# A two-layer diffusion block with mixture of experts: context key and query columns made directly transposed, one modulation product moved between the layers, and a leaner hand-over at the end of the experts

## The chip, the cores and the metric

The kernel runs on one core of one Trainium2 chip. The metric is the device time of one execution in microseconds (us); lower is better. Everything is fp32. The profile is one execution of the same program, read from its trace.

## What is computed

256 latent tokens (x) and 256 context tokens (ctx), 1024 wide, go through two layers. In the last layer only the latent tokens are carried on. Cut to what matters here:

```
for l in range(2):
    mod, modc = silu(c) @ w_ada[l] + b_ada[l], silu(c_ctx) @ w_ada[l] + b_ada[l]   # 6 x 1024 each
    h, hc = rmsnorm(x) * (1 + mod[1]) + mod[0], the same for ctx with modc
    qa, ka, va, qb, kb, vb, uc = split(h @ w_in[l]);  the same for hc
    rotary embedding of qa, ka, qb, kb, for the latent tokens only
    o_a = differential attention (4 heads), o_b = windowed attention with sinks (4 heads), o_c = conv module of uc
    x = x + mod[2] * (concat(o_a, o_b, o_c) @ w_out[l]);  layer 0: the same for ctx
    h2 = rmsnorm(x) * g_ffn * (1 + mod[4]) + mod[3]
    y = 16 experts (1024 -> 512 -> 1024), 2 per token
    x = x + mod[5] * y
out = rmsnorm(x, g_final)
```

The keys and queries of the context tokens get no rotary embedding: they go from the product to the attention as they are.

## The kernel before

Work on the five engines is written out by hand and kept in step by semaphores; between stages all engines but SyncE pass a barrier (`barrier`: drain the engine, raise `phase`, wait until four engines have done so; `pass_barrier` on GpSimd is the same without the drain). One layer is this series of stages:

1. **Columns of h** (barrier 1). VectorE scales X by the row norms into YS. TensorE transposes YS, eight groups named `nT`; VectorE and ScalarE evict them with scale and shift into HT, which holds h with features on the partitions.
2. **Input products** (barrier 2), in the order of `in_jobs`: uc, ka, b, va, qa. Weight segments of 2 MB lie in a ring of six slots. A job of ka, b or qa is one tile of 128 tokens: eight matmuls with HT stationary and 512 weight columns moving. Its result has tokens on the partitions, but scores need features there, so it is put into a staging tile ST (by VectorE with the rotary embedding for tiles 0 and 1, by ScalarE's L949 as a plain copy for the context tiles 2 and 3), transposed by TensorE (`transposes`, L1682, one job later) and copied by ScalarE (`copy_T`, L918) into kT or qT. Jobs of uc are made the other way round: weights stationary, HT moving, features on the partitions.
3. **Attention** (barrier 3): units of one query tile and one pair of heads, 24 in layer 0 and 12 in layer 1. `attention_steps` writes the order out: scores S two units ahead, the transposes T of the probabilities (L1770), the outputs O of the unit before. Between S and T `fill` puts up to three steps of "dense" work: in layer 0 first the three modulation products (1, 0), (1, 1), (1, 2) of layer 1 ("A" steps, `ada_part`, four matmuls of 128x32 on 128x512 each, eight steps a product), then the output products ("W") of query tiles whose heads are done. Units 0 to 2 carry product (1, 0), units 3 to 5 carry (1, 1), units 6 to 8 carry (1, 2); W begins at unit 9.
4. **Routing** (barrier 4), and then the **experts** (barrier 5): per expert 6 MB of weights through nine slots, and a loop over blocks of 32 tokens. GpSimd gathers block n (L830) and scatters the result of block m (L838). Each scatter first waits for the result, then copies its list of rows (L836), then starts its DMA.
5. **Combine**: ScalarE loads the scattered rows, two DMAs for each token tile (L1069), VectorE adds the two, multiplies by the gate and adds to X (L1589, L1591, L1593), ScalarE and GpSimd make the norms, VectorE makes YS of the next layer (L1139).

A modulation product (l, q) makes 2048 of the 6144 modulation columns for both conditions. Its weights come in four loads of 2 MB, `front_units`; VectorE adds the bias (`mod_rows`, L1115), GpSimd stores the rows to DRAM (`store_mod`) and other engines load them back. (1, 1) holds the attention gate and the shift of the second norm of layer 1, which are first needed after barrier 2 of layer 1.

SyncE's queue has all weight loads in order. At the end of layer 0 it issues the last expert's loads, two gate loads (L704), then waits for the combine's second tile, and then loads layer 1's segments (L650). A load also waits until its slot was freed by TensorE.

Of the kernel before, what the change touches and what calls it, by code (L numbers as in the profile page):

```python
# [43 lines left out]
EXTRA = 3 * GROUPS - RING  # L44

# [75 lines left out]
def bank_plan():  # L121
# [13 lines left out]
    for l in range(DEPTH):  # L135
        nq = TILES if l == 0 else 2
        for g in range(8):
            if l == 0 and g == 4:
                for key in (("par",), ("cw",), ("ada", 0, 0), ("modc", 0)):
                    put(key)  # L140
            put(("nT", l, g))
        prev = None
        for job in in_jobs(l):
# [3 lines left out]
            prev = job if job[0] in ("ka", "b", "qa") else None  # L147
# [65 lines left out]

def quad_after(l, job):
# [7 lines left out]
def front_units(l):  # L222

    out = [("ada", 0, j) for j in range(4)] if l == 0 else []
# [6 lines left out]
    if l == 0:  # L231
        out += [("ada", 1, j) for j in range(4 * QUADS)]
# [13 lines left out]
def attention_steps(l):  # L246
# [4 lines left out]
    dense = ([("A", q) for q in range(QUADS)] if l == 0 else []) + [("W", i, h) for i in range(nq - 1) for h in range(OUT_N)]  # L251
# [41 lines left out]
def hybrid_moe_kernel(nc, A):  # L293
# [4 lines left out]
    with ctx:  # L298
# [69 lines left out]
        def mst_of(key):  # L368
# [4 lines left out]
            return acc[:, 0 if q == 0 else 1, 0:CHUNK]  # L373
# [189 lines left out]
        def bar(l, k):  # L563
            return 5 * l + k
# [6 lines left out]
        MODS = [(l, q) for l in range(DEPTH) for q in range(QUADS)]  # L571

        def bias_of(n):
            return bias0 if n == 0 else bias12[:, n % 2] if n < QUADS else G[:, 1, 0:CHUNK]
# [70 lines left out]
        def _(sp):  # L645
# [8 lines left out]
            for l in range(DEPTH):  # L654
                for name in front_units(l):
                    if name[0] == "ada":
# [48 lines left out]
                if l < DEPTH - 1:  # L705

                    sp.wait_ge(y_in[1], 32 * (l + 1))
# [3 lines left out]
        def _(pool):  # L711
# [48 lines left out]
            for l in range(DEPTH):  # L760
# [28 lines left out]
                if l == 0:  # L789
                    pool.wait_ge(mod_sb, QUADS + 1)  # L790
                    load_bias(QUADS + 1)
                    pool.wait_ge(mod_sb, QUADS + 2)
                    store_mod(QUADS + 1)
                    load_bias(QUADS + 2)
                else:
                    load_ffn_rows(l)
                for i in range(nq):
                    if l == 0 and i == 1:
                        pool.wait_ge(mod_sb, QUADS + 3)
                        store_mod(QUADS + 2)  # L800
                        pool.wait_ge(ab_done, 2)
                        for q in range(1, QUADS):
                            pool.wait_ge(mod_out[1, q], 64)
# [16 lines left out]
                def gather(n, r, made_=0):  # L820
# [4 lines left out]
                    if isinstance(n, int):  # L825
# [1130 lines left out]
```

## Time and profile before

| | us |
|---|---|
| median of 3 runs | 1211.78 (1206.96 to 1214.02) |
| the profiled execution, its own time | 1216.56 |
| its span in the trace | 1214.8 |
| TensorE busy, share of the span | 971.6, 80% |
| TensorE weight loads | 529.7, 44% |
| VectorE busy | 464.1, 38% |
| ScalarE busy | 257.1, 21% |
| GpSimd busy | 224.5, 18% |
| mean granted TensorE clock | 0.897 of full speed |
| DMA | 317.92 MB, mean 262 GB/s |

A busy share is a mean over stages with different limits. The stages lie as follows: layer 0 until about 360 us up to its routing, its experts until 690, combine and layer 1's start until 725, layer 1's products and attention until about 900, its experts until 1190, and the final combine.

### The profile page before, as it was taken

What the parts mean: (1) busy time and instruction counts of PE and PEld (TensorE: products, weight loads), DVE (VectorE), ACT (ScalarE), POOL (GpSimd) and SP (SyncE); (2) the same over time, 40 slices, a digit from 0 to 9 for tenths busy, and PEclk for the clock granted to TensorE, in tenths of its full rate; (3) what the DMA queues carried; (4) which work ended last, traced back from release to release, by engine and by line L of the source; (5) the groups of instructions that cost most, each with busy time, mean ns of one, the idle gap of its engine ahead of it and who ended that gap; (6) DMA issues with size and microseconds to landing.
All of it is one profiled execution on the core that took longest, in us unless ns stands there. A gap on an engine that the chain in (4) does not pass through costs nothing. (4 is left out here: it accounts for less than half of the span.)

```text
span 1214.8 us, 23396 instructions
## 1 busy us (share of the span) xinstructions
PE 971.6 (80%) x8536; PEld 529.7 (44%) x8537; DVE 464.1 (38%) x1008; ACT 257.1 (21%) x497; POOL 224.5 (18%) x364
## 2 busy tenths in 40 slices
PE   3899999999889399999989429998887397755880
PEld 1344444355446255555545225543554254322440
DVE  1159505555535433333323166606633422211233
ACT  2100112343312022222212020113511122111110
POOL 2100000121001124333433230000000123211331
PEclk9699999999987599999989869999988598877895
DMA  9966612995003668999999196115007299999983
GB/s 368 391 263 259 260 54 81 364 398 206 1 1 149 255 257 332 413 370 414 422 420 419 44 386 237 70 69 208 1 1 285 107 393 412 411 421 425 415 361 127
DMA packets 52747, 317.92 MB, mean 262 GB/s; under 512 B 6984, under 2 KB 7064, under 8 KB 30160
## 3 DMA queue, kind: packets, MB, share of 16 engines
q1 hardware_dynamic: 40144, 284.70, 58.3%
q0 software_dynamic: 9344, 20.54, 4.6%
q10 hardware_dynamic: 3200, 11.86, 2.6%
q8 instruction: 41, 0.67, 0.2%
q14 instruction: 18, 0.15, 0.0%
HBM read 309.13 MB, written 12.65 MB: 265 GB/s over the span
## 5 line engine op out<-in xcount | busy, mean ns | idle before, releaser
L1608 PE MATMUL ps<-ring,HT 128*128 128x512 f32 (+1 forms) x672 | 299.2, 598 | 8.1 <-DVEq L554 5.7
L1608 PE MATMUL ps<-ring,area 128*32 128x256 f32 x3936 | 248.9, 404 | 42.4 <-DMA ring<-in_w 30.1
L1608 PE MATMUL ps<-area 128*32 128x256 f32 (+5 forms) x1896 | 216.3, 390 | 25.6 <-DVE area L1516 11.5
L1608 PEld LDWEIGHTS ps<-ring,HT 128*128 128x128 f32 x672 | 127.1, 195 | 156.0 <-issue 148.9
L1608 PEld LDWEIGHTS ps<-ring,area 128*32 128x32 f32 x3936 | 133.3, 116 | 130.2 <-issue 48.7
L1608 PEld LDWEIGHTS ps<-area 128*32 128x32 f32 (+2 forms) x1896 | 119.7, 136 | 49.3 <-issue 15.4
L1534 DVE COPY area<-ps 128x256 f32<-128x256 f32 x65 | 27.6, 425 | 249.6 <-PE ps L1850 249.6
L1608 PE MATMUL ps<-HT,area 128*32 128x256 f32 x704 | 86.7, 402 | 25.0 <-DMA area<-in_w 21.5
L1063 ACT ACTIVATE area<-ps 64x256 f32<-64x256 f32 x63 | 23.8, 378 | 377.3 <-PE ps L1608 377.3
L830 POOL DMA_INDIRECT area<-h_rows,area x68 | 71.2, 1048 | 118.7 <-DVEq L554 62.7
L1063 ACT ACT_TABLE_LOAD x63 | 80.8, 1283 | 38.5 <-DVEq L1527 37.4
L838 POOL DMA_INDIRECT expert_rows<-area x64 | 65.6, 1025 | 56.4 <-POOL area L836 56.4
L1167 DVE SCALAR_TENSOR_TENSOR area<-area,CW 128x512 f32<-128x512 f32 (+1 forms) x120 | 68.8, 614 | 3.9
L1608 PEld LDWEIGHTS ps<-HT,area 128*32 128x32 f32 x704 | 45.0, 116 | 54.3 <-issue 32.3
L1556 DVE COPY area<-ps 128x256 f32 (+1 forms) x63 | 26.8, 425 | 96.2 <-PE ps L1608 75.1
L836 POOL COPY area<-area 128x1 int32 x64 | 15.2, 237 | 213.8 <-DVE area L1556 210.7
L1608 PE MATMUL ps<-ring,SC 128*32 128x512 f32 x384 | 48.3, 643 | 5.0 <-DMA ring<-in_w_ada 4.8
L727 POOL TENSOR_SCALAR ms<-ss 128x1 f32<-128x1 f32 (+1 forms) x22 | 10.6, 482 | 208.8 <-DVE ss L1324 136.1
L997 ACT ACTIVATE area<-ps 128x512 f32<-128x512 f32 (+1 forms) x48 | 25.2, 526 | 106.5 <-PE ps L1770 69.8
L1670 PE MATMUL ps<-cst,area 128*128 128x128 f32 x64 | 12.6, 383 | 42.3 <-DVE area L1139 40.7
L1608 PE MATMUL ps<-HT,ring 128*128 128x512 f32 (+1 forms) x128 | 43.8, 504 | 2.4 <-POOLq L732 1.2
L1286 DVE TENSOR_REDUCE mx<-ps 128x2 f32<-128x1024 f32 (+1 forms) x36 | 37.6, 1044 | 18.2 <-PE ps L1608 17.8
(197 smaller groups left out, 813.0 us busy)
## 6 DMA issues: line engine op xcount, KB each, us to landing
ring<-in_w SPq DMA_DIRECT2D x66, 2048.0 KB
ring<-in_w_ada SPq DMA_DIRECT2D x24, 2048.0 KB
ring<-in_w_in SPq DMA_DIRECT2D x10, 2048.0 KB
HT<-in_w SPq DMA_DIRECT2D x10, 2048.0 KB
area<-in_w SPq DMA_DIRECT2D x10, 2048.0 KB
area<-in_w SPq DMA_DIRECT2D x20, 1024.0 KB
ring<-in_w_out SPq DMA_DIRECT2D x4, 2048.0 KB
area<-expert_rows ACTq DMA_DIRECT2D x12, 512.0 KB, 6.6
```

The costliest lines, as they stand in the source:

```text
L727: link(g.tensor_scalar(m_, s_, 1.0 / n, EPS, ALU.mult, ALU.add))
L830: pool.indirect_dma_start(xg[:, r * NW:(r + 1) * NW], None, h2_rows, bass.IndirectOffsetOnAxis(ap=at_, axis=0), bounds_check=routed(l) * N ...
L836: g.tensor_copy(sidx[r], TS[:, bass.ds(m, 1)]).then_inc(sidx_set[l], 1)
L838: pool.indirect_dma_start(y_rows, bass.IndirectOffsetOnAxis(ap=sidx[r], axis=0), ym[:, r * NW:(r + 1) * NW], None, bounds_check=2 * routed ...
L997: taken(s.activation(aT[:, k % 2, 0:kw], bank(key)[:, 0:kw], ACT.Identity), key)
L1063: s.activation(sg[0:64, :], ps[0:64, B_W13, 0:NW], ACT.Silu).then_inc(si_rdy[l], 1)
L1167: v.scalar_tensor_tensor(dst, src, w, dst, ALU.mult, ALU.add)
L1286: v.tensor_reduce(mx[:, b], pair[:, :, 0:kw], AX.X, ALU.max)
L1534: v.tensor_copy(xT.rearrange("p a s -> p (a s)"), ps[:, B_XT, 0:NW]).then_inc(xt_rdy[l], 1)
L1556: v.tensor_copy(ym[:, bass.ds(m % 2 * NW, NW)], ps[:, B_W2, 0:NW]).then_inc(y_rdy[l], 1)
L1608: return t_.matmul(out, lhsT, rhs, start=first, stop=last_)
L1670: last = t_.transpose(bank(key)[:, a * 256 + t * P:a * 256 + (t + 1) * P], YS[:, 2 * cnd + t, (kk + a) * P:(kk + a + 1) * P], ident)
```

## The change

Six edits, in the order of the program:

- ka and qa of context tiles are no longer products of one token tile each. A job with t = 2 or 3 (`by_column`) now makes two blocks of 128 features for all 256 context tokens: weights stationary, HT moving, 16 matmuls of N = 256 in the place of eight of N = 512. ScalarE copies the result straight into kT or qT. No staging, no transposes. That is six jobs: ka 2 and 3 in both layers, qa 2 and 3 in layer 0.
- Modulation product (1, 1), named LATE, is taken out of layer 0's attention. Its first three loads are put on SyncE's queue behind the last expert and the gates, before the wait for the combine's second tile, its fourth load behind that wait. TensorE computes it at the start of layer 1's code, ahead of the `nT` transposes, VectorE adds its bias behind the `nT` evictions, GpSimd stores it before barrier 2 of layer 1. Bank 7 is kept for it, and `nT` of layer 1 uses seven banks.
- A scatter copies its list of rows before it waits for the result. Because the list must not change under a running scatter, it waits first for the scatter two before it.
- The first pair of the gather and scatter loop is written out.
- GpSimd passes barrier 5 without a drain.
- The combine loads each token tile with one DMA in the place of two.

```diff
+LATE = (1, 1)
...
+        if l == LATE[0]:
+            put(("ada",) + LATE, bank=7)
...
-            put(("nT", l, g))
+            put(("nT", l, g), range(8 if l == 0 else 7))
...
+def by_column(job):
+
+    return job[0] in ("ka", "qa") and job[1] >= S_LAT // P
+
+
+def is_staged(job):
+
+    return job[0] in ("ka", "b", "qa") and not by_column(job)
...
-    out = [("ada", 0, j) for j in range(4)] if l == 0 else []
+    out = [("ada", 0, j) for j in range(4)] if l == 0 else [("ada",) + (LATE[0], 4 * LATE[1] + j) for j in range(4)]
...
-    dense = ([("A", q) for q in range(QUADS)] if l == 0 else []) + [("W", i, h) for i in range(nq - 1) for h in range(OUT_N)]
+    dense = ([("A", q) for q in range(QUADS) if q != LATE[1]] if l == 0 else []) + [("W", i, h) for i in range(nq - 1) for h in range(OUT_N)]
...
             for l in range(DEPTH):
                 for name in front_units(l):
+                    if l and name == ("ada", l, 4 * LATE[1] + 3):
+
+                        sp.wait_ge(y_in[1], 16 * l)
...
-                if l < DEPTH - 1:
-
-                    sp.wait_ge(y_in[1], 32 * (l + 1))
...
+                else:
+                    pool.wait_ge(mod_sb, MODS.index(LATE) + 1)
+                    store_mod(MODS.index(LATE))
+                    pool.wait_ge(mod_out[LATE], 64)
                 pass_barrier(bar(l, 2))
...
                 def scatter(m, r):
 
-                    hold(pool, y_rdy[l], m + 2, pool_passed)
+                    if not isinstance(m, int):
+                        hold(pool, scat[l][r], pool.snap(sent) * 8, pool_passed)
                     g.tensor_copy(sidx[r], TS[:, bass.ds(m, 1)]).then_inc(sidx_set[l], 1)
                     hold(pool, sidx_set[l], m + 1, pool_passed)
+                    hold(pool, y_rdy[l], m + 2, pool_passed)
...
+                for r in range(2):
+                    gather(PEEL + r, r, r)
+                    scatter(r, r)
...
-                barrier(pool, bar(l, 5))
+                pass_barrier(bar(l, 5))
+                if l + 1 == LATE[0]:
+                    load_bias(MODS.index(LATE))
...
-                    elif seg in ("ka", "qa") and t >= 2:
+                    elif by_column(job):
                         wait_made(act, key)
-                        st_free(job)
-                        taken(s.activation(stg, bank(key), ACT.Identity), key)
+                        b0 = 2 * (t - S_LAT // P)
+                        taken(s.activation((qT if seg == "qa" else kT)[:, b0:b0 + 2, S_LAT:TOK], bank(key).rearrange("p (b t) -> p b t", b=2), ACT.Identity), key)
...
-                    for k in range(2):
-                        act.dma_start(Y[:, i, k], y_v[:, i, k]).then_inc(y_in[i], 16)
+                    act.dma_start(Y[:, i], y_v[:, i]).then_inc(y_in[i], 16)
...
+                if l == LATE[0]:
+                    mod_rows(LATE)
                 barrier(dve, bar(l, 1))
...
+                if l == LATE[0]:
+                    ada(*LATE)
                 for q in range(8):
...
-                    for k in range(KD):
+                    if by_column(job):
+                        for b in range(2):
+                            cols = slice((2 * (t - S_LAT // P) + b) * P, (2 * (t - S_LAT // P) + b + 1) * P)
+                            for k in range(KD):
+                                last = mm(bank(key)[:, b * S_CTX:(b + 1) * S_CTX], unit[:, k, cols], HT[:, k, S_LAT:TOK], k == 0, k == KD - 1)
+                    for k in range(KD if not by_column(job) else 0):
```

The change moves rows of the written order at two places that matter. The first is TensorE in layer 0's attention, units 6 to 8 (`ps<-ring,SC 32x512` are "A" steps, the next row of transposes are the T of that unit). Before:

```order
L1628 MATMUL ps<-cst,area 128x128 x4
L1608 MATMUL ps<-area 128x512 x2
L1608 MATMUL ps<-ring,SC 32x512 x12
L1770 MATMUL ps<-cst,area 128x128 x4
L1608 MATMUL ps<-area 128x64 x8
L1608 MATMUL ps<-area 128x512 x2
L1608 MATMUL ps<-ring,SC 32x512 x12
L1770 MATMUL ps<-cst,area 128x128 x4
```

The same place now:

```order
L1648 MATMUL ps<-cst,area 128x128 x4
L1628 MATMUL ps<-area 128x512 x2
L1798 MATMUL ps<-cst,area 128x128 x4
L1628 MATMUL ps<-area 128x64 x8
L1628 MATMUL ps<-area 128x512 x2
L1798 MATMUL ps<-cst,area 128x128 x4
L1628 MATMUL ps<-area 128x128 x4
```

Units 0 to 5 still carry two products; units 6, 7 and 8 have nothing between scores and transposes.

The second place is SyncE's queue from the end of layer 0's experts. Before:

```order
L704 DMA gate<-mod_rows 128x1024 x2
L650 DMA ring<-in_w_in 128x8x512 x5
L650 DMA ring<-in_w_out 128x8x512 x2
L690 DMA ring<-in_w 128x4096 x2
L692 DMA ring<-in_w 128x2x2048
```

Now:

```order
L720 DMA gate<-mod_rows 128x1024 x2
L663 DMA ring<-in_w_ada 128x2x2048 x4
L663 DMA ring<-in_w_in 128x8x512 x5
L663 DMA ring<-in_w_out 128x8x512 x2
L706 DMA ring<-in_w 128x4096 x2
```

Four loads of 2 MB stand ahead of layer 1's first segment; only the fourth of them waits for the combine.

## Rows read from the trace of the kernel before

**Rows 1.** Stretches: us, busy PE, PEld, DVE, ACT, POOL, then clock, DMA share, GB/s

```profile
212.00:269.00 57.00, 52.55 (x375) 24.78 (x376) 29.73 (x65) 20.74 (x57) 10.71 (x21) 0.97 0.99 377
640.00:667.00 27.00, 24.63 (x402) 13.72 (x401) 8.13 (x20) 6.65 (x8) 10.08 (x16) 1.00 1.01 419
690.00:719.00 29.00, 0.00 (x0) 0.00 (x0) 15.72 (x15) 4.60 (x8) 8.61 (x7) 0.50 0.72 272
740.00:797.00 57.00, 56.48 (x166) 28.97 (x167) 35.42 (x85) 6.30 (x17) 0.00 (x0) 1.00 0.32 118
```

**Rows 2.** Timeline (start, us, engine): last scatters and combine's loads, layer 0, then 1

```profile
685.51 0.18 POOL L836 COPY area<-area 128x1 int32 x1 [1.69 <-DVEq L1582]
686.58 0.99 POOL L838 DMA_INDIRECT expert_rows<-area  x1 [0.89 <-POOL area L836]
688.63 0.98 POOL L838 DMA_INDIRECT expert_rows<-area  x1 [0.86 <-POOL area L836]
697.57 4.04 ACTq L1069 DMA_DIRECT2D area<-expert_rows  x8
...
1188.32 0.98 POOL L838 DMA_INDIRECT expert_rows<-area  x1 [0.86 <-POOL area L836]
1194.93 1.79 ACTq L1069 DMA_DIRECT2D area<-expert_rows  x4
```

**Rows 3.** Timeline: the combine of layer 0 and the start of layer 1

```profile
702.67 1.23 DVE L1589 TENSOR_TENSOR area<-area 128x1024 f32<-128x1024 f32 x1 [17.66 <-DMA area<-expert_rows]
705.13 18.19 SPq L650 DMA_DIRECT2D ring<-in_w_in  x5
719.14 5.23 PE L1670 MATMUL ps<-cst,area 128*128 128x128 f32 x32 [35.79 <-DVE area L1139]
721.09 3.91 DVE L1149 TENSOR_SCALAR HT<-ps,AB 128x256 f32<-128x256 f32 x8
```

**Rows 4.** Timeline: a staged job's transposes, and the products of N 256 and 512

```profile
141.48 0.60 PE L1682 MATMUL ps<-cst,area 128*128 128x128 f32 x4
141.92 7.03 PE L1608 MATMUL ps<-ring,HT 128*128 128x512 f32 x16
...
725.60 14.08 PE L1608 MATMUL ps<-HT,ring 128*128 128x256 f32 x64 [1.22 <-POOLq L732]
739.94 13.97 PE L1608 MATMUL ps<-ring,HT 128*128 128x512 f32 x32 [0.26 <-issue]
```

**Rows 5.** Timeline: the end of layer 0's input products and the first scores

```profile
210.06 1.23 DVE L1273 TENSOR_TENSOR HT<-area 128x1024 f32<-128x1024 f32 x1 [8.81 <-PE ps L1608]
...
212.13 1.99 PE L1608 MATMUL ps<-area 64*128 64x512 f32 x8 [0.76 <-ACTq L554]
```

**Rows 6.** Timeline of TensorE, layer 0's attention, T of unit 5 to T of unit 8

```profile
248.10 1.06 PE L1770 MATMUL ps<-cst,area 128*128 128x128 f32 x8 [0.29 <-issue]
...
252.98 2.78 PE L1608 MATMUL ps<-ring,SC 128*32 128x512 f32 x24
...
267.83 0.63 PE L1770 MATMUL ps<-cst,area 128*128 128x128 f32 x4 [0.29 <-issue]
```

**Rows 7.** Timeline of TensorE, layer 1's attention, T of unit 5, unit 7 and unit 8

```profile
860.16 1.09 PE L1770 MATMUL ps<-cst,area 128*128 128x128 f32 x8
...
871.36 0.66 PE L1770 MATMUL ps<-cst,area 128*128 128x128 f32 x4 [2.05 <-DVE area L1304]
871.85 3.31 PE L1608 MATMUL ps<-area 128*128 128x128 f32 x12
...
876.02 0.60 PE L1770 MATMUL ps<-cst,area 128*128 128x128 f32 x4
```

**Rows 8.** Timeline: a quarter of a modulation product at low clock, a bias addition

```profile
33.74 3.64 PE L1608 MATMUL ps<-ring,SC 128*32 128x512 f32 x16 [1.94 <-DMA ring<-in_w_ada]
...
247.87 0.69 DVE L1115 TENSOR_TENSOR area<-ps,area 128x512 f32<-128x512 f32 x1 [0.31 <-PE ps L1608]
```

**Rows 9.** DMA issues: the stores of h2 (issues, KB each, us to landing)

```profile
h_rows<-area ACTq DMA_DIRECT2D x6, 512.0 KB, 2.6
```

More of the change, by code:

```diff
@@ L146, in bank_plan @@
                 put(("inT", l) + prev)
-            prev = job if job[0] in ("ka", "b", "qa") else None
+            prev = job if is_staged(job) else None
             if quad_after(l, job):
@@ L231, in front_units @@
     if l == 0:
-        out += [("ada", 1, j) for j in range(4 * QUADS)]
+        out += [("ada", 1, 4 * q + j) for q in range(QUADS) if q != LATE[1] for j in range(4)]
     return out + [("out", h) for h in range(OUT_N)]
@@ L372, in mst_of @@
                 return gate[:, 0 if q == 0 else 1, 0:CHUNK]
-            return acc[:, 0 if q == 0 else 1, 0:CHUNK]
+            return bias12[:, 1] if key == LATE else acc[:, 0 if q == 0 else 1, 0:CHUNK]
         YS = cut(TILES * D, 0).rearrange("p (t d) -> p t d", t=TILES)
@@ L568, in hybrid_moe_kernel @@
         ones = cst[:, C_ONE:C_ONE + P]
-        MODS = [(l, q) for l in range(DEPTH) for q in range(QUADS)]
+        MODS = [(l, q) for l in range(DEPTH) for q in range(QUADS) if (l, q) != LATE] + [LATE]
         def bias_of(n):
-            return bias0 if n == 0 else bias12[:, n % 2] if n < QUADS else G[:, 1, 0:CHUNK]
+            return bias0 if n == 0 else bias12[:, n % 2] if n < QUADS else G[:, 1, 0:CHUNK] if MODS[n] != LATE else bias12[:, 0]
         IN_COL = {"qa": 0, "ka": 1, "va": 2, "b": 3, "uc": 4}
@@ L798, in _ @@
                     if l == 0 and i == 1:
-                        pool.wait_ge(mod_sb, QUADS + 3)
-                        store_mod(QUADS + 2)
+                        pool.wait_ge(mod_sb, QUADS + 2)
+                        store_mod(QUADS + 1)
                         pool.wait_ge(ab_done, 2)
-                        for q in range(1, QUADS):
-                            pool.wait_ge(mod_out[1, q], 64)
+                        pool.wait_ge(mod_out[1, 2], 64)
                         load_ffn_rows(l)
@@ L824, in gather @@
                     at_ = gidx[r]
-                    if isinstance(n, int):
+                    if isinstance(n, int) and n < PEEL:
                         at_ = TG[:, n:n + 1]
@@ L896, in _ @@
                 barrier(act, bar(l, 1))
-                staged = [j for j in in_jobs(l) if j[0] in ("ka", "b", "qa")]
+                staged = [j for j in in_jobs(l) if is_staged(j)]
                 def st_free(job):
@@ L1151, in _ @@
                     taken(last, key)
+                if l == LATE[0]:
+                    mod_rows(LATE)
                 barrier(dve, bar(l, 1))
-                staged = [j for j in in_jobs(l) if j[0] in ("ka", "b", "qa")]
+                staged = [j for j in in_jobs(l) if is_staged(j)]
                 def conv_taps():
@@ L1587, in _ @@
                 for i in range(nq):
-                    dve.wait_ge(y_in[i], 32 * (l + 1))
+                    dve.wait_ge(y_in[i], 16 * (l + 1))
                     v.tensor_tensor(Y[:, i, 0], Y[:, i, 0], Y[:, i, 1], ALU.add)
@@ L1633, in ada_part @@
                 key = ("ada", l, q)
-                x = slot(0, ("ada", l, 4 * q + k // 2))
+                row = l if (l, q) == LATE else 0
+                x = slot(row, ("ada", l, 4 * q + k // 2))
                 if k == 0:
@@ L1637, in ada_part @@
                 if k % 2 == 0:
-                    arrived(pe, 0, ("ada", l, 4 * q + k // 2))
+                    arrived(pe, row, ("ada", l, 4 * q + k // 2))
                 for c in range(4):
@@ L1695, in channel_sums @@
                     made(last, (name, l))
-                staged = [j for j in in_jobs(l) if j[0] in ("ka", "b", "qa")]
+                staged = [j for j in in_jobs(l) if is_staged(j)]
                 prev, jobs = None, in_jobs(l)
```

12 lines of the change are left out of this document (4 added, 8 removed).

## The prediction

> **What bounds the kernel now.** I read the stretches first. In the input products TensorE is busy 56.48 of 57 us, and in layer 0's attention with its A steps 52.55 of 57, while VectorE has 29.73 there; in the experts' stretch from 640 to 667 both TensorE (24.63 of 27) and the DMA engines (share 1.01) are full; from 690 to 719 TensorE does nothing [rows 1]. So an instruction taken from TensorE counts in the products and the attention of either layer, and the combine is a free place for TensorE work. Then I read the timeline at the hand-overs. From the start of layer 0's last scatter at 688.63 to the combine's first load at 697.57 nothing is computed, and VectorE starts to add at 702.67, TensorE to transpose at 719.14 [rows 2, 3]. These two stretches, and the same at the end of layer 1, are pure latency: what is taken from their chain counts in full. The experts themselves I take as shifted, not changed: their bytes, products and number of blocks stay the same, and a start that is earlier for weights and products alike passes through to their end.
>
> **Columns of the context tiles.** A job's eight matmuls of N = 512 stand as 16 records in 7.03 us, or 32 in 13.97. A job now has 16 matmuls of N = 256, 32 records; 64 such records, also with ring weights stationary and HT moving, took 14.08 us, so 32 take 7.04 [rows 4]. The product costs the same. The transposes took 0.44 us of a period (from 141.48 to 141.92) [rows 4]. Four of the six jobs' transposes (ka 2 and 3 of both layers) stand between products: 4 x 0.44 = 1.8 us. The other two stand at the end of layer 0's products. There the first scores start at 212.13, released by ScalarE, which copies the last two transposes. Without them the stage ends with VectorE's product into HT, 210.06 + 1.23 = 211.29, and a barrier: 0.7 us less [rows 5]. ScalarE's spared copies are off the path. Sum 2.5 us; bounds 1.5 (VectorE's conv chain holds the end of layer 1's products) and 3.0.
>
> **The modulation product, taken out.** Units 6 to 8 lose their A steps, 64 matmul records, of which 24 take 2.78 us: 7.4 us [rows 6]. That is all TensorE time, but with the filler gone the softmax chain of VectorE and ScalarE shows. Layer 1 runs the same three units without a filler: from T of unit 5 to T of unit 8 it takes 876.02 - 860.16 = 15.86 us, with 2.05 us of waiting for VectorE and a stretch in which the clock was low (12 matmul records in 3.31 us). Layer 0 takes 267.83 - 248.10 = 19.73 [rows 6, 7]. But layer 0 also has the transposes and copies of its modulation columns here and one bias addition of 0.69 us on VectorE [rows 8], for which I add 0.9. So 19.7 becomes 16.8: 3.0 us gained of 7.4. Bounds: 7.4 if nothing shows, and 1.0 if the additions fall wholly on VectorE's chain and the low clock lasts longer. The 8 MB that leave this stage gain nothing by themselves: it is nearly full of transfers (share 0.99), but TensorE fills most of it too [rows 1].
>
> **The modulation product, put in.** The stretch from 697.6 to 719.1 takes it. TensorE's clock is at 0.50 there, the lower of its two levels [rows 1]; a quarter of a product, two k steps, took 3.64 us at low clock [rows 8]. Three quarters take 10.9 us from 697.6, so until 708.5. Their weights can be there: in SyncE's queue they follow the last expert's loads and the gates, and the slots they need are those of the expert before the last but one, so all of it is behind TensorE's last product, before 685.5 [rows 2]. The last quarter is issued when the combine's second tile has landed, 705.13 [rows 3]. The stretch from 690 to 719 moved 272 GB/s x 29 us = 7.9 MB, and nothing before about 698.7, so 0.39 MB/us [rows 1]. By 705.1 that is 2.5 of the combine's 4.2 MB; with half the engines each, both have moved the missing 1.7 at 713.8, the last quarter's 2.1 are through at 714.8 and seen some 1.3 us later, 716.1. (The first tile's MB takes 2.7 of the 5.1 us from its issue to VectorE's start; I put 1.1 ahead of it and 1.3 behind it.) With 3.6 us of work TensorE ends at 719.7, 0.6 behind the present start of the transposes, most of which VectorE's evictions cover (3.91 us back to back from 721.09 [rows 3]). The first segment of uc comes 2.1 MB later, 5.9 MB after 705.1, seen at about 721.5, and is needed at 725.6. What is not covered is VectorE's bias addition behind the evictions: they end at 725.0, the barrier falls at 725.6 [rows 4], and 0.8 us more with the drain moves it to 725.9. With a part of the late transposes I take 0.6 us lost. Bounds: 0.3 and 4 (the second rival).
>
> **The end of the experts.** The last scatter but one now has its list in place: from 685.51 to the DMA at 686.58 were 1.07 us, which go [rows 2]. The very last one still copies behind it. In layer 1 it is the real one, and it gains the same, since its list is copied while the last block is computed. So 1.05 us in each layer. In the loop the scatter is off the path, and its new wait stops nothing: VectorE's copy of the result, for which the scatter waited before, waits for the same older scatter itself. The pair that is written out is covered alike. **The drain:** a scatter's data must land; from the last scatter's start to the first load are 8.9 us in layer 0 and 6.6 in layer 1 [rows 2]. No row shows its landing or the drain. The nearest store to DRAM, that of h2, lands 2.6 us after its issue [rows 9]; with the scatter's own 0.98 that is 3.6, so 5.3 and 3.0 us remain in which the drain lies with whatever else, a longer landing above all. Its bounds are 0 and these. 
>
> **The combine's loads.** Eight issues took 4.04 us and four took 1.79, some 0.5 each [rows 2], while the tile's second half must flow behind its first in either form. One issue less ahead of a tile: 0.2 us a layer, bounds 0 and 0.5.
>
> The Trainium skill (DMA: Bandwidth & Descriptors, section "Anatomy of one DMA") gives a DMA 2.0 us plus its bytes at 436 GB/s. An estimate from that page is 4.4 us for 1 MB against 5.1 measured from the first issue to VectorE's start, which would make the gain 0.7 us in each layer and the sum 1.0 larger.
>
> **The sum.** 2.5 + 3.0 - 0.6 + 2 x (1.05 + 1.0 + 0.2) = 9.4 us. The profiled execution took 1216.56, 4.8 above the median; from it 1207.2, and from the median of 1211.78, **1202.4 us**. A measurement of this kernel tells about 0.5% (6 us) from no change.
>
> **The rivals.**
>
> *More goes than I took.* The bare units lose all 7.4 us, and the drain is all that is unexplained (8.3 us in place of 2.0 together). Then 9.4 + 4.4 + 6.3 = 20.1, or 1191.7 us; half of it gives 1197. For it: nothing else is named in those 8.9 us. Against it: layer 1's own bare units wait for VectorE, and scattered rows may land later than a plain store.
>
> *The product in the combine gates layer 1.* Its last quarter is seen at 719 and not at 716, because the combine's loads go first. Then the transposes start at 722.6, the products 3 to 3.5 us later than I took; 1205.9 us. For it: my time for it already ends 0.6 us late, with VectorE's cover of one or two. Against it: SyncE's loads did flow in this stretch at a mean of 272 GB/s with the idle part counted in [rows 1].
>
> *Slower: all four quarters load behind the barrier.* Place: SyncE's queue ahead of the combine. If a slot comes free only at the barrier, 4.2 MB of combine and 8.4 MB of weights start at 698.7 and end at 731.0, seen at 732.3; the last quarter ends at 735.9, the transposes (5.23 us [rows 3]) at 741.1, and the barrier falls near 742.3, 16.7 us later than now. With the rest of my sum that is 1202.4 - 0.6 + 16.7 = 1218.5 us. It costs from the point at which the last quarter is seen later than 715.5, and it eats the whole gain at about 726. Against it: those slots' products are over before 685.5 [rows 2].
>
> **How the numbers follow.** Forecast 0.58, its own range 1197 to 1207; more goes 0.16; gated 0.18; slower 0.08. Faster by over 0.5% is below 1205.7: 0.49 of the forecast, all of the first rival, 0.07 of the second, 0.72. Same: the 0.09 and 0.11 left of these, 0.20. Slower 0.08. The range reaches from 1194, between the forecast and the whole of the first rival, to 1211, behind the second; some 0.08 lies below and 0.10 above.
>
> **What would show it.** Right: product periods of 7.0 us without transposes; 16 to 17.5 us from T of unit 5 to T of unit 8 in layer 0; A steps of layer 1 between the barrier and 720 with the `nT` transposes at once behind; the barrier's side of the last scatter shorter by a us or more. Wrong: `nT` waiting for a `w_ada` load, 128x256 products above 0.23 us a record, no shorter gap between the last scatter and the combine's loads.

## The result and the profile after

| | before | changed |
|---|---|---|
| median, us | 1209.24 (1202.85 to 1215.26, 9 runs) | 1197.79 (1192.55 to 1202.57, 9 runs) |
| the profiled execution, its own time | 1216.56 | 1197.05 |
| its span | 1214.8 | 1195.3 |
| mean granted TensorE clock | 0.897 | 0.906 |

The ratio is 0.9903 (95%: 0.9884 to 0.9922): 11.7 us faster (9.4 to 14.0 by the interval), where 9.4 were forecast. The sum holds; several of its terms do not, and they cancel in part.

The stretches that answer to [rows 1] (us, busy PE, PEld, DVE, ACT, POOL, then clock, DMA share, GB/s): layer 0's attention, the experts, the combine with layer 1's start, layer 1's products.

```profile
207.00:260.00 53.00, 45.43 (x312) 23.59 (x312) 29.32 (x66) 21.15 (x57) 11.06 (x21) 0.97 0.92 353
628.00:655.00 27.00, 23.23 (x362) 12.56 (x358) 6.82 (x18) 5.90 (x8) 9.27 (x15) 0.94 1.01 421
680.00:712.00 32.00, 14.82 (x97) 5.98 (x97) 21.39 (x25) 8.36 (x16) 12.17 (x13) 0.71 0.98 367
726.00:783.00 57.00, 56.22 (x195) 34.91 (x194) 35.70 (x85) 5.11 (x15) 0.00 (x0) 1.00 0.36 132
```

The combine is no longer empty on TensorE: 14.82 us of 32, and its DMA share is 0.98 where it was 0.72.

The columns, timeline of TensorE in layer 0: jobs of 7.07 us with nothing of their own between them; the 0.60 us of transposes belong to the staged job before.

```profile
93.81 7.07 PE L1628 MATMUL ps<-HT,ring 128*128 128x256 f32 x32
100.72 0.60 PE L1705 MATMUL ps<-cst,area 128*128 128x128 f32 x4
101.15 7.07 PE L1628 MATMUL ps<-HT,ring 128*128 128x256 f32 x32
...
205.61 1.23 DVE L1293 TENSOR_TENSOR HT<-area 128x1024 f32<-128x1024 f32 x1 [8.89 <-PE ps L1628]
206.92 1.99 PE L1628 MATMUL ps<-area 64*128 64x512 f32 x8 [1.35 <-DVEq L567]
```

From VectorE's product to the first scores are 1.31 us, 2.07 before [rows 5]. The barrier is now released by VectorE, not by ScalarE's copies.

The attention without the product, T of unit 5, 7 and 8 [rows 6]:

```profile
241.35 1.06 PE L1798 MATMUL ps<-cst,area 128*128 128x128 f32 x8 [0.38 <-issue]
...
253.32 0.66 PE L1798 MATMUL ps<-cst,area 128*128 128x128 f32 x4 [2.05 <-DVE area L1324]
253.81 3.68 PE L1628 MATMUL ps<-area 128*128 128x128 f32 x12
257.42 0.73 PE L1628 MATMUL ps<-cst 128*128 128x128 f32 x4
257.99 0.60 PE L1798 MATMUL ps<-cst,area 128*128 128x128 f32 x4
```

16.64 us from unit 5 to unit 8 (19.73 before, 16.8 forecast), with the same 2.05 us of waiting for VectorE that layer 1 showed [rows 7].

The hand-over of layer 0, timeline of all engines [rows 2, 3]:

```profile
671.10 1.03 POOL L853 DMA_INDIRECT expert_rows<-area  x1 [2.77 <-DVE area L1576]
673.25 0.42 DVE L1576 COPY area<-ps 128x256 f32 x1 [2.34 <-PE ps L1628]
674.57 0.99 POOL L853 DMA_INDIRECT expert_rows<-area  x1 [2.24 <-DVEq L1602]
676.76 0.18 POOL L850 COPY area<-area 128x1 int32 x1 [1.20 <-DMA expert_rows<-area]
677.96 0.98 POOL L853 DMA_INDIRECT expert_rows<-area  x1 [1.01 <-issue]
680.17 3.02 ACTq L1087 DMA_DIRECT2D area<-expert_rows  x4
680.20 7.30 PE L1628 MATMUL ps<-ring,SC 128*32 128x512 f32 x48 [7.79 <-POOLq L745]
687.02 1.23 DVE L1609 TENSOR_TENSOR area<-area 128x1024 f32<-128x1024 f32 x1 [13.34 <-DMA area<-expert_rows]
690.35 0.37 SPq L663 DMA_DIRECT2D ring<-in_w_ada  x1
700.49 3.64 PE L1628 MATMUL ps<-ring,SC 128*32 128x512 f32 x16 [13.00 <-DMA ring<-in_w_ada]
704.18 0.55 POOL L741 TENSOR_TENSOR rstd<-ms,half 128x1 f32<-128x1 f32 x1
704.42 3.78 PE L1693 MATMUL ps<-cst,area 128*128 128x128 f32 x32 [0.29 <-issue]
709.06 0.68 DVE L1133 TENSOR_TENSOR area<-ps,area 128x512 f32<-128x512 f32 x1
711.90 15.53 PE L1628 MATMUL ps<-HT,ring 128*128 128x256 f32 x64 [3.70 <-POOLq L567]
711.95 0.15 POOL L786 MEMSET area<- 128x60 f32 x1 [7.22 <-POOLq L567]
```

From the last scatter (677.96) to the first load are 2.2 us, 8.9 before. But VectorE is done at 709.7 and the barrier ahead of layer 1's products opens only at 711.9, and what released it is GpSimd's sequencer, 7.2 us after GpSimd's last instruction. The experiments have two questions to answer. Is the drain worth all of the 6.7 us? And does moving the product pay?

Single executions of a program differ by some us, because stretches of low clock fall differently. So I cut each trace at ten marks, all read from the timeline, and compare pieces. S: first scores; G: first gather; C: last copy of an expert's result; load: the combine's first load; add: VectorE's first addition; uc: layer 1's first input product.

| us | before | changed | changed, again | product back | product back, again | drain back |
|---|---|---|---|---|---|---|
| start to S | 212.13 | 206.92 | 210.70 | 207.50 | 206.20 | 207.49 |
| S to G | 204.87 | 198.68 | 195.48 | 197.51 | 200.04 | 194.62 |
| G to C | 267.59 | 267.65 | 267.82 | 268.34 | 267.78 | 268.09 |
| C to load | 12.98 | 6.92 | 6.77 | 6.06 | 6.08 | 13.50 |
| load to add | 5.10 | 6.85 | 6.00 | 5.78 | 5.76 | 6.75 |
| add to uc | 22.93 | 24.88 | 24.98 | 24.55 | 24.55 | 23.09 |
| uc to S, layer 1 | 113.74 | 114.46 | 114.79 | 113.01 | 113.04 | 113.10 |
| S to G | 118.59 | 117.58 | 118.26 | 118.53 | 117.29 | 118.27 |
| G to C | 228.41 | 227.14 | 230.32 | 227.39 | 230.09 | 226.94 |
| C to load | 8.59 | 3.79 | 3.78 | 3.78 | 3.78 | 7.93 |
| load to end | 19.87 | 20.43 | 20.10 | 20.05 | 20.39 | 19.82 |

In a second execution of the same program the pieces at the hand-overs repeat within 0.2 us (load to add within 0.9); the long ones with attention or experts scatter by up to 4 us. Between programs that do not differ in the piece the scatter is larger: with the moved product, C to load of layer 0 runs from 6.8 to 8.1 us, start to G from 402 to 408. The trace of before is a single one, and its execution took 7.3 us more than the median.

### The profile page after: what moved, and what is told of

Its sections match the earlier page's. It is cut to its first block and busy times, and to the rows that moved or that the text cites. A ratio compares the mean times of both kernels' runs of the same rounds, so it can differ in the third digit from the quotient of the medians.

```text
span 1195.3 us, 23583 instructions
## 1 busy us (share of the span) xinstructions
PE 965.3 (81%) x8608; PEld 542.7 (45%) x8609; DVE 463.2 (39%) x1008; ACT 253.4 (21%) x491; POOL 223.8 (19%) x364
## 5 line engine op out<-in xcount | busy, mean ns | idle before, releaser
L1628 PE MATMUL ps<-ring,HT 128*128 128x512 f32 (+1 forms) x576 | 256.7, 598 | 8.4 <-DVEq L567 5.3
L1628 PEld LDWEIGHTS ps<-ring,HT 128*128 128x128 f32 x576 | 109.4, 195 | 137.1 <-issue 130.5
L1628 PE MATMUL ps<-HT,ring 128*128 128x256 f32 (+1 forms) x320 | 87.3, 433 | 4.8 <-POOLq L567 3.7
L1628 PEld LDWEIGHTS ps<-HT,ring 128*128 128x128 f32 x320 | 61.9, 196 | 27.9 <-issue 15.8
L1628 PE MATMUL ps<-ring,SC 128*32 128x512 f32 x384 | 48.9, 652 | 25.9 <-DMA ring<-in_w_ada 17.6
L1582 DVE SCALAR_TENSOR_TENSOR area<-area,ps 64x256 f32<-64x256 f32 x63 | 43.2, 685 | 2.0
```

Of the source, the lines that this page charges most:

```text
L1582: v.scalar_tensor_tensor(gg[0:64, :].rearrange("s (c p) -> s p c", c=NCH), sg[0:64, :].rearrange("s (p c) -> s p c", c=NCH), TW[0:64, bass ...
L1628: return t_.matmul(out, lhsT, rhs, start=first, stop=last_)
```

## The experiments

All ratios are to the kernel before on the same chip; the changed kernel has 0.9903.

**The drain, put back.**

```diff
-                pass_barrier(bar(l, 5))
+                barrier(pool, bar(l, 5))
```

> The changed kernel with one word put back: GpSimd drains before it signals the barrier behind the experts, in both layers. Theory A: the drain behind the scatters is most of what was between the last scatter and the combine's first load, 6.7 us of it in layer 0 (8.9 before, 2.2 now) and 4.1 in layer 1 (6.6 before, 2.5 now). Then this kernel shows gaps of 6.5 to 9 and of 6.5 us again and takes 8 to 10 us more than the changed one, about 1206.5 us. Theory B: the drain costs 1 us a layer as I had put it, and the shorter gap comes from elsewhere (the scatter's list, the clock, one load in the place of two): gaps of 3.2 to 3.5 us, about 1199.8 us.

Measured: 1204.51 us, ratio 0.9958 (0.9943 to 0.9973), so 0.55% or 6.6 us slower than the changed kernel. Its timeline at the end of layer 0 and of layer 1:

```profile
674.73 0.98 POOL L853 DMA_INDIRECT expert_rows<-area  x1 [1.01 <-DMA expert_rows<-area]
683.70 3.48 ACTq L1087 DMA_DIRECT2D area<-expert_rows  x4
...
713.55 0.15 POOL L786 MEMSET area<- 128x60 f32 x1 [5.38 <-DVEq L567]
...
1173.15 0.98 POOL L853 DMA_INDIRECT expert_rows<-area  x1 [2.26 <-DVEq L1602]
1179.78 0.91 ACTq L1087 DMA_DIRECT2D area<-expert_rows  x2
```

The gaps are back to 9.0 and 6.6 us: the drain costs 6.8 us in layer 0 and 4.1 in layer 1 (2.5 are left without it). Theory A holds in both places, but the total is 6.6 and not 8 to 10. The table shows where the rest is: with the drain, add to uc is 23.09 and not 24.9, and uc to S 113.1 and not 114.5 to 114.8. The barrier ahead of layer 1's products is then opened by VectorE (the MEMSET row). Without the drain behind the scatters, the next drain of GpSimd takes longer and holds that barrier. GpSimd's four small bias loads stand ahead of that drain in both kernels, so they are not the cause.

**That next drain, taken away too.**

```diff
-                barrier(pool, bar(l, 1))
+                pass_barrier(bar(l, 1))
```

> The changed kernel, with GpSimd's drain taken from the barrier ahead of the input products too (both layers). In layer 1 GpSimd's last instruction ends at 704.7 and VectorE's at 709.7, and the barrier opens at 711.9. Theory A: GpSimd's drain, with its four bias loads of 64 KB still on their way, holds the barrier: it opens within 0.5 us of VectorE's end, 1.5 to 2 us sooner, about 1196 us. Theory B: something else opens it (the drain of VectorE or ScalarE, code loading): the same 2.2 us stay, 1197.8 us.

Measured: 1197.46 us, ratio 0.9891 (0.9874 to 0.9907), no more than the changed kernel by what can be told. The barrier did open 0.2 us behind VectorE's addition (add to uc 23.03, uc to S 113.01): 1.9 us were gained there as in theory A, and 1.5 more as clock behind it. But S to G of layer 1 went from 117.6 and 118.3 to 122.4. The timeline of the barrier behind layer 1's attention, where GpSimd's one remaining drain stands (first the last norm, then what follows the barrier):

```profile
888.67 1.01 POOL L741 TENSOR_TENSOR rs<-ms,half 128x4 f32<-128x4 f32 x1
897.51 7.97 PE L1628 MATMUL ps<-ring,HT 128*128 128x512 f32 x14 [4.74 <-POOLq L567]
897.56 0.52 POOL L821 MEMSET area<- 128x512 f32 x1 [7.88 <-POOLq L567]
```

And the same place with both drains kept:

```profile
891.37 1.01 POOL L741 TENSOR_TENSOR rs<-ms,half 128x4 f32<-128x4 f32 x1
897.77 7.13 PE L1628 MATMUL ps<-ring,HT 128*128 128x512 f32 x16 [2.30 <-DVEq L567]
897.78 0.52 POOL L821 MEMSET area<- 128x512 f32 x1 [5.40 <-DVEq L567]
```

Call the cost that a left-out drain leaves behind its debt. With the debt paid earlier, GpSimd is ready in less than 5.40 us and VectorE opens the barrier; in the changed kernel it is ready in less than 3.55. With the debt unpaid it needs 7.88 and holds everyone. The cost of the drain is not removed by leaving out a drain: it goes to the next one. All four kernels of this study without the drain at barrier 1 have it: S to G of layer 1 is 122.40, 121.45, 123.40 and 120.82 us in them, and 117.3 to 118.6 in the ten others. In this kernel about 2.4 us of this are the barrier (TensorE waits 4.74 us for 2.30). The rest lies behind it: from the barrier to the first gather are 48.8 us there and 47.1 in the kernel with both drains, and TensorE's granted clock in the first 4 us behind the barrier is 0.57 and 1.00. Three of the four kernels show this stretch of low clock, and one execution of the changed kernel does too (48.9 us), so it is not due to the debt alone.

**The product, put back into the attention.** Cut to the core (SyncE's wait, the banks and GpSimd's stores go back with it):

```diff
-LATE = (1, 1)
+LATE = (9, 9)
...
-    out = [("ada", 0, j) for j in range(4)] if l == 0 else [("ada",) + (LATE[0], 4 * LATE[1] + j) for j in range(4)]
+    out = [("ada", 0, j) for j in range(4)] if l == 0 else []
```

> The changed kernel with modulation product (1, 1) put back into layer 0's attention, all else as changed. Theory A: the move is worth 2.4 us, as the prediction had it (3.0 gained in the attention, 0.6 lost in the combine): about 1200.2 us. Theory B: it is worth nothing, since what the attention gains (T of unit 5 to T of unit 8 in 16.6 for 19.7 us) is given back ahead of layer 1's products, where first load to first uc product went from 28.0 to 31.7 us: about 1197.5 us, with 19.5 to 20 us at the first place and 28 to 29 at the second.

Measured: 1194.54 us, ratio 0.9878 (0.9859 to 0.9897). That is less than either theory gives. Both kernels were run once more, on one chip.

> The changed kernel with the modulation product back in layer 0's attention, once more. Theory A: the move costs as much as it gives, in stages 3.1 gained in the attention against 3.7 lost (0.9 to 2 at the end of the scatters, 1 at the first addition, 0.3 and 1.4 behind it): ratio to the changed kernel within 0.25% of 1. Theory B: the move costs 3 us, as the medians of the first time had it: 0.25% or more faster than the changed kernel. Theory C, the prediction's: 2.4 us slower.

> The changed kernel once more, beside the three below on the same chip: about 1197.5 us, ratio to before 0.990. Theory A (what its stages show is how it works): last copy of a result to the combine's first load 6.8 to 8.5 us in layer 0 and 3.8 in layer 1, first addition to first uc product 24.9. Theory B (they were a matter of one execution): these change by over 1 us.

Measured: product back 1194.02 us, 0.9867 (0.9841 to 0.9893); changed 1198.52, 0.9904 (0.9885 to 0.9923). The forecast of 2.4 us gained by the move is refuted; the kernel is faster without it, by 0.25% the first and 0.37% the second time. The pieces show the mechanism. The attention does give 3.1 us: T of unit 5 at 241.82 and T of unit 8 at 261.55 with the product back, 19.73 us as before, for 16.64. From C to S of layer 1 the move costs 3.4 us: 153.1 and 152.5 for 149.4 and 149.4. That is 0.8 at C to load, 0.7 at load to add, 0.4 at add to uc, 1.6 at uc to S (means of the two executions). Two other kernels with the moved product that do not touch the end of layer 0's experts have 7.9 and 8.1 us at C to load, so the loss there can be 2.0 and the whole some 4.6. The pieces make the move worth between nothing and 1.5 us lost. By the medians it costs 3 to 4.5 us, with an interval of some 2.5 us on the mean of both. What is left stays open. It lies ahead of the experts: from the start to the first gather the two executions with the product back took 405.0 and 406.2 us, the changed kernel 405.6 and 406.2, so the 3.1 us of the attention do not show in the whole stretch. Two further kernels with the product back took 409.0 and 413.6 us there.

Where the 3.4 us come from: the window from 660 to 680, the last 20 us ahead of the load, reads first in the changed kernel and then with the product back

```profile
660.00:680.00 20.00, 11.14 (x180) 5.73 (x172) 4.49 (x11) 2.04 (x3) 7.10 (x11) 0.93 0.75 307
```

```profile
660.00:680.00 20.00, 10.86 (x176) 5.60 (x168) 4.49 (x11) 2.04 (x3) 7.09 (x11) 0.87 0.04 12
```

The moved product's three loads fill the DMA engines (307 GB/s for 12) exactly while the last scatters must land and be waited for. And the 1.6 us are granted clock: TensorE runs the last quarter and the transposes from 700.5 to 708.2, then waits 3.7 us for the barrier. Windows of the changed kernel before and behind the barrier:

```profile
706.00:711.00 5.00, 2.20 (x21) 1.96 (x18) 3.74 (x8) 3.44 (x8) 0.00 (x0) 1.00 1.05 387
711.00:716.00 5.00, 4.10 (x12) 3.43 (x13) 0.00 (x0) 0.00 (x0) 2.34 (x6) 0.66 1.05 387
```

The clock is at its upper level (2.4 GHz) after the product and drops towards 1.2 GHz just as the products start: the first job takes 15.53 us for 14.08 before [rows 4]. The pause alone is not the whole condition. All five traces in which the last quarter ran right ahead of the transposes and a pause of 2.5 to 4.3 us followed show the drop (uc to S 114.5 to 115.5 us). With the same work and a pause of 1.45 us it is absent. So it is with a pause of 2.46 us and no quarter, and with one of 3.10 us and the quarter over 12.9 us ahead of the transposes (113.0 to 113.1 us in each). In return the transposes themselves took 3.78 us, 5.23 before [rows 3].

**The fourth load ahead of the wait.**

```diff
-                    if l and name == ("ada", l, 4 * LATE[1] + 3):
+                    if l and name == ("uc",):
```

> The changed kernel with the fourth load of the moved product no longer behind the wait for the combine's second tile; uc's load takes that wait. Theory A: TensorE's wait of 13 us for this quarter goes, its transposes start with VectorE's first tile, and the barrier ahead of layer 1's products opens no sooner than GpSimd's drain allows, 711.9 now: gain 0 to 1 us, and the combine's first addition comes later, since the load competes with it (7.5 to 9 us from the first load in place of 6.9): about 1198 us. Theory B: the quarter is what holds layer 1's start: the stretch from first addition to first uc product, 24.9 us, falls to 23 or less, and the total by 1.5 to 2 us, about 1196 us.

Measured: 1195.22 us, ratio 0.9878 (0.9857 to 0.9900), perhaps 3 us better than the changed kernel, though the intervals overlap. TensorE did the product in one piece while nothing else needed it:

```profile
683.85 9.84 PE L1628 MATMUL ps<-ring,SC 128*32 128x512 f32 x64 [9.47 <-POOLq L745]
706.53 5.36 PE L1693 MATMUL ps<-cst,area 128*128 128x128 f32 x32 [12.85 <-DVE area L1157]
715.04 0.15 POOL L786 MEMSET area<- 128x60 f32 x1 [7.22 <-POOLq L567]
```

Add to uc did not fall (25.22), since GpSimd's drain opens the barrier, its 7.22 us behind the last norm as in the changed kernel. Load to add was 5.94, no worse. What was gained is the clock: uc to S is 113.01. Against it C to load was 8.51, and from the last scatter to the load were 3.17 us for 2.2. These pieces add up to nothing (1.6 and 0.5 gained, 1.7 and 0.3 lost), so the 3 us of the medians are not shown by them. As stages go, neither theory is right: B had the place wrong, and A had no room for the clock.

**Lists of their own for the last two scatters, with the two edits above; and the same with the product back.**

```diff
-        sidx = [cut(1).bitcast(i32) for _ in range(2)]
+        sidx = [cut(1).bitcast(i32) for _ in range(4)]
...
                 for r in range(2):
-                    scatter(pool.snap(sent) + r, r)
+                    g.tensor_copy(sidx[2 + r], TS[:, bass.ds(pool.snap(sent) + r, 1)]).then_inc(sidx_set[l], 1)
...
```

> The changed kernel with three things more: the fourth load of the moved product ahead of the wait, no drain of GpSimd ahead of the input products, and lists of their own for the last two scatters, copied before either waits. Theory A: in layer 0 the last scatter no longer waits for the landing of the one two before it, last copy to first load falls from 6.8 to 8.5 us to 4.5 or less; first addition to first uc product falls from 24.9 to 22 to 23; together 4 to 5 us, about 1193 us. Theory B: the scatters' landing, slowed by the product's weights in the same DMA engines, holds the barrier in place of the list, and uc's weights the products: 7 and 24 us again, 1196 us.

> The same without the moved product (it is back in layer 0's attention): no drain of GpSimd ahead of the input products, and lists of their own for the last two scatters. Theory A: last copy to first load falls from 6.1 us to 4 in layer 0, the rest as with the product back (first load to addition 5.7, then 24.2): 2 us under that kernel, about 1193 us. Theory B: the landing holds the barrier, 6 us again, about 1195 us.

Measured: 1200.66 us, 0.9917 (0.9893 to 0.9941), and 1199.44 us, 0.9910 (0.9889 to 0.9931). Neither beats the changed kernel. The end of layer 0 in the first, then in the second:

```profile
672.73 1.03 POOL L853 DMA_INDIRECT expert_rows<-area  x1 [2.78 <-DVE area L1581]
676.30 0.99 POOL L874 DMA_INDIRECT expert_rows<-area  x1 [2.23 <-DVEq L1607]
677.59 0.98 POOL L874 DMA_INDIRECT expert_rows<-area  x1 [0.31 <-issue]
683.08 3.44 ACTq L1092 DMA_DIRECT2D area<-expert_rows  x4
```

```profile
682.59 0.99 POOL L873 DMA_INDIRECT expert_rows<-area  x1 [2.63 <-DVEq L1606]
683.88 0.97 POOL L873 DMA_INDIRECT expert_rows<-area  x1 [0.30 <-issue]
686.09 2.43 ACTq L1091 DMA_DIRECT2D area<-expert_rows  x4
```

The last scatter follows its neighbour by 1.3 us in both. With the product's loads in flight the load then starts 5.5 us behind it, without them 2.2 us; C to load is 8.09 and 4.82. So theory B holds with the moved product (the landing is what is late, and the list only hid it), theory A without it (6.07 to 4.82, where it had 4). Both kernels also carry the unpaid drain. Their S to G of layer 1 is 3 to 5 us longer, and that eats what was gained.

**The product back and no drain at barrier 1**, the one edit of each together:

> The changed kernel with the modulation product back in layer 0's attention, and GpSimd's drain taken from the barrier ahead of the input products. With the product back the kernel took 1194.5 us, and there the barrier of layer 1 opened 6.9 us after GpSimd's last instruction and 1.5 us or so after VectorE's. Theory A: the drain held it there too, and the scatters' landing is not slowed by the product's loads: first addition to first uc product falls from 24.6 to 23 us, 1193 us in all. Theory B: without the product other work (the transposes with their evictions, from 701.7 to 708) sets the barrier and nothing is gained: 1194.5 us.

Measured: 1199.25 us, 0.9920 (0.9893 to 0.9946). Add to uc is 24.21 for 24.55, near theory B. But here the transposes took 6.6 us at low clock (704.9 to 711.5) and the barrier opened 0.6 us behind VectorE's last eviction of them. The kernel with lists of their own and the product back has the same barrier without a drain, transposes of 5.5 us, and 23.19: what theory A had. The debt is at its new place again: S to G 121.45. Neither theory had this.

**The scatter's old order.**

```diff
-                    if not isinstance(m, int):
-                        hold(pool, scat[l][r], pool.snap(sent) * 8, pool_passed)
+                    hold(pool, y_rdy[l], m + 2, pool_passed)
                     g.tensor_copy(sidx[r], TS[:, bass.ds(m, 1)]).then_inc(sidx_set[l], 1)
                     hold(pool, sidx_set[l], m + 1, pool_passed)
-                    hold(pool, y_rdy[l], m + 2, pool_passed)
...
                 for r in range(2):
+                    hold(pool, scat[l][r], pool.snap(sent) * 8, pool_passed)
                     scatter(pool.snap(sent) + r, r)
```

> The changed kernel with the old order of a scatter (wait for the result, copy the list of rows, start the DMA), all else as changed. Theory A: the copy and its wait, 1.05 us a layer, come back behind the last scatter but one in layer 0 and behind the last one in layer 1: last copy of a result to its scatter 2 us for 1.3, about 1199.5 us. Theory B: in layer 0 the last scatter waits for the landing of the scatter two before it (1.2 us idle now), which hides the copy, so only layer 1 loses 0.7 us: about 1198.5 us. The experts' loop stays as long, 267 to 268 and 227 us, in either.

Measured: 1199.77 us, 0.9917 (0.9895 to 0.9940); by the medians not to be told from the changed kernel. Layer 1's C to load is 4.48 for 3.79: 0.7 us. In layer 0 it is 8.21, inside what kernels with the moved product show (6.8 to 8.5), and the last scatter again waits for the one two before it:

```profile
676.11 0.99 POOL L851 DMA_INDIRECT expert_rows<-area  x1 [0.89 <-POOL area L849]
679.06 0.18 POOL L849 COPY area<-area 128x1 int32 x1 [1.96 <-DMA expert_rows<-area]
680.10 0.98 POOL L851 DMA_INDIRECT expert_rows<-area  x1 [0.86 <-POOL area L849]
```

Theory B. The loop is as long as ever (268.01 and 226.86).

**Two loads for a tile again.**

```diff
-                    act.dma_start(Y[:, i], y_v[:, i]).then_inc(y_in[i], 16)
+                    for k in range(2):
+                        act.dma_start(Y[:, i, k], y_v[:, i, k]).then_inc(y_in[i], 16)
...
-                    dve.wait_ge(y_in[i], 16 * (l + 1))
+                    dve.wait_ge(y_in[i], 32 * (l + 1))
```

> The changed kernel with the combine's tiles loaded by two DMAs each again, all else as changed. In layer 0 the first load to VectorE's first addition took 5.1 us before and 6.9 now, in layer 1 5.3 and 5.5. Theory A: one DMA in the place of two gives 0.2 us a layer, and layer 0's 6.9 comes from the three weight loads of the moved product that are still queued there: 6.8 to 7.2 and 5.5 to 5.9 us here, total 0.4 us up, within the measurement's grain. Theory B: the single DMA of 1 MB is itself what takes longer: 5.1 to 5.5 us in both layers here, and 1 to 1.5 us less in total.

Measured: 1197.17 us, 0.9906 (0.9883 to 0.9928): no difference. Load to add is 6.59 and 5.16 us with two DMAs; with one it is 6.85 and 5.52, again 6.00 and 5.56. Where nothing competes, in layer 1, all twelve kernels with one DMA have 5.34 to 5.64, the two with two 5.16 and 5.33: the single DMA is some 0.2 us slower, not faster. Layer 0's 6 to 6.9 us come from the neighbours, since with the product back it is 5.8.

**The columns, undone.** ScalarE's copy into the staging tile comes back with it.

```diff
-    return job[0] in ("ka", "qa") and job[1] >= S_LAT // P
+    return False
```

> The changed kernel with the context tiles' keys and queries made row by row again (staged and transposed), all else as changed. Theory A: 0.44 us for each of four jobs and 0.7 at the end of layer 0's products come back, 2.5 us: about 1200.3 us. Theory B: at the end of layer 0's products and in layer 1 other work (VectorE's conv chain, the barrier) sets the end, so 1 us or less comes back: about 1198.5 us.

Measured: 1200.55 us, 0.9929 (0.9899 to 0.9959), 0.26% slower than the changed kernel with a wide interval: 3.1 us for 2.5 forecast. The pieces are surer. The end of layer 0's products is as before (207.84 to 209.91, 2.07 us), and uc to S of layer 1 is 115.46 for 114.46 and 114.79, where the sum had 0.9. All three have the drop of the clock in them. Without it are before, 113.74, and the kernels with 113.0: 0.7 us.

## Why the prediction was right, and where it was not

**Columns, 2.5: right.** 0.76 at the exit of layer 0's products (0.7 forecast), 0.7 to 1.0 in layer 1's products (0.88); in layer 0's products the jobs show no transposes between them. That they save 0.9 us there is read from the rows and was not measured by itself.

**The product taken out, 3.0: right** (3.1 from T of unit 5 to T of unit 8), including the reason, VectorE's chain showing through. In the whole stretch up to the first gather it does not show, as said above.

**The product put in, 0.6 lost: wrong.** The last quarter went much as worked out: it was seen 10.1 us after its issue (11 forecast), and add to the transposes went from 16.5 to 17.4 us. At the barrier that is 0.2 us, as the kernel with the drain back shows (add to uc 23.09 for 22.93). (The three quarters took 7.3 us and not 10.9; they waited for nothing and held nothing up.) The step that failed is "their weights can be there", which had no price. They were there, and the scatters and the combine's loads paid for it: 0.8 us or more at C to load, 0.7 at load to add. The other missed part is the drop of the clock at the start of layer 1's products, 1.6 us. The whole move is worth nothing at best, and not 2.4.

**The scatter's list, 1.05 in each layer: half right.** 0.7 in layer 1; in layer 0 nothing that can be seen, because the last scatter there carries no new result (none is copied after 673.25) and waits for a landing.

**The drain, 1.0 in each layer: the term that was mis-sized.** It measured 6.8 and 4.1 us, 10.9 in place of 2.0. I took the low end of its bounds "because GpSimd has nothing but a finished queue to drain"; the 8.9 us had no other named content, and the bound from the store of h2, 5.3 and 3.0, was too low even at its upper end. Some 3.3 of it came back, 1.8 at the next barrier and 1.5 as clock behind it, so the net is 7.6 us by the pieces and 6.6 by the medians. The prediction had no step for this debt. What the drain waits for stays open: the landing of the last scatter was waited for ahead of it in either kernel.

The Trainium skill (VectorE: DVE Perf Modes, section "The DRAIN you can't avoid") has drains of about 12 ns on all engines, in the preamble and postamble. The drain of this case is not of that kind: behind indirect DMAs the runs show 4.1 and 6.8 us for GpSimd's.

**The combine's loads, 0.2 in each layer: wrong sign**, some 0.2 us slower in layer 1. The Trainium skill (DMA: Bandwidth & Descriptors, section "Anatomy of one DMA") gives 2.0 us plus the bytes at 436 GB/s for a DMA that GpSimd issues, an estimate of 4.4 us for 1 MB. The prediction used it for loads that ScalarE issues. From the first issue to VectorE's start the single DMA took 5.3 to 5.6 us, and two of half the size 5.2 and 5.3 together, so the 0.7 us of gain that it gave did not come.

Counted by pieces, with the means of both executions of the changed kernel: 2.5 for the columns and 3.1 for the attention, 10.9 at the two C to load; less 1.3 at load to add, 2.0 at add to uc, 1.8 at uc to S (beside the columns' 0.9) and 0.4 at the end. That makes 11.0 of the 11.7 us. It leaves out what the long pieces differ by: up to the first gather alone the two traces are 11 us shorter than the one execution of before, for 4.7 that the columns and the attention give there. That 9.4 was near is luck, since a drain worth 4.6 us net more than taken stood against a moved product worth 2.7 less or more, and a list and loads worth 2 less. The rival "more goes than I took" was right that the drain was underrated (8.3 us in place of 2.0, 10.9 measured) and wrong on the attention.

## What to carry to other kernels

A drain can be debt: leaving it out moves its cost to the engine's next drain, so put that one where the engine has time. Here it would be right behind the barrier ahead of layer 1's products, where GpSimd is idle for some 110 us in the changed kernel. This was not tried. A free engine is not a free stage: the combine had TensorE idle, but its DMA engines and the wait for the last scatters were the path, and 6 MB of loads ahead of them cost what the work saved. Of the versions run, the change without the moved product is the fastest, 1194.0 us against 1198.5 on the same chip, though the pieces explain at most 1.5 us of it.

## What the runs showed of the hardware

- From the end of the last scatter, whose landing is waited for in either case, to the next stage are 8.0 and 5.6 us with a GpSimd drain and 1.2 and 1.5 us without. Left out, the next drain opens its barrier 6.9 to 7.9 us after GpSimd's last instruction, even if it stands some 210 us later with ordinary DMAs of the same engine in between. Where one has been made, the following one was done in less than 3.55 us.
- From the start of the last indirect scatter to the release of the next stage were 2.2 us with nearly idle DMA engines (19 GB/s in the 20 us around it) and 5.5 us beside weight loads (350 GB/s).
- TensorE's work ahead of the transposes gave them the upper clock (3.78 us in place of 5.23, and 1.00 granted from 706 to 711), and behind a pause of 3.7 us it fell at the start of the products (0.66 from 711 to 716). With no quarter right ahead, pauses of 2.5 and 3.1 us cost nothing.
